# Dense products walked from the last column to the first: moving operand and PSUM bank with a step of -1

## The chip, the cores and the metric

The kernel runs on one core of a Trainium2 chip. The metric is the device time of one execution in microseconds (us), the median of the runs of a kernel. Of the core's engines, TensorE multiplies (PE in the profile's rows; PEld is its loading of weights), VectorE is DVE, ScalarE is ACT, GpSimd is POOL, and SyncE (SP) starts the DMAs.

## The reference

The reference is a two-layer encoder trunk over 512 tokens of 1024 features with 16 learned tokens put in front, 528 in all. Each layer is wrapped by two feed-forward networks with half a residual each:

```python
def swiglu(x, w_gate, w_up, w_down):
    return (jax.nn.silu(x @ w_gate) * (x @ w_up)) @ w_down
...
for layer in range(DEPTH):
    h = h + FFN_RESIDUAL * swiglu(rmsnorm(h, norm_ff1[layer]), ff1_w_gate[layer], ...)
    hn = rmsnorm(h, norm_mix[layer])
    # layer 0: z = hn @ w_in; gated short convolution || diagonal state-space model + GLU; concat @ w_out
    # layer 1: qkv = hn @ w_qkv; sliding-window attention, 16 query heads over 4 key heads; @ w_o
    h = h + mix
    h = h + FFN_RESIDUAL * swiglu(rmsnorm(h, norm_ff2[layer]), ff2_w_gate[layer], ...)
```

The feed-forward weights are 1024 x 2816 and 2816 x 1024, everything is float32, and the last layer drops the 16 learned tokens.

## The kernel before

**Layout.** Activations lie with features on the 128 partitions and tokens along the free dimension: `h`, `xh`, `xl` hold 8 feature tiles of 528 tokens, `act_h` and `act_l` 12. A row of `xh`, `xl`, `act_h`, `act_l` is 576 elements of 4 bytes, of which 528 are used. A value is kept as a rounded part (`xh`, `act_h`, `wh`) and the rest (`xl`, `act_l`, `wl`), in the type `float32r`, and a product is three matmuls: high weights by high values, high weights by low values, low weights by high values (the loop over `q`). `float32r` products go through TensorE once; the few products of plain float32 tiles are built as more than one pass.

**One dense product.** The weights are the stationary operand, a block of 128 x 128. The moving operand is a row of tokens, and the result goes to a bank of `ps`, the 8 banks of 512 float32. There are three choices of columns: `ALL` is two halves of 264 tokens in two banks, with the loop over `hf` inside the loop over `q`, so that halves alternate; `REAL` is the 512 real tokens at column 16; `FRONT` is 512 at column 0, where the operands of the last feed-forward network lie. A chain over the feature tiles adds into the same bank, then the last matmul raises `tile_full`. Every matmul loads its weights again, so there is one LDWEIGHTS record for each MATMUL record.

**Where they are.** `mm3` (its matmul is line 799) does nearly all of the four feed-forward networks: gate, up and down products. Lines 844 and 859 are the first two products of the kernel, issued while the inputs are still being split. Line 1015 is the input projection of layer 0, line 1029 its GLU, line 1057 its output projection, line 1126 the query projection of layer 1, lines 1227 and 1265 its output projection. The key and value projection (line 1076) has tokens as the stationary operand and weights as the moving one. Transposes, token sums, the state-space and the attention matmuls have lines of their own.

**What sets the order.** All is written out by hand, with semaphores. SP loads weight units of 16 blocks into one of two halves of `raw`; ACT rounds them to `wh` (line 1276), DVE takes the difference `wl` (line 1563); PE waits for `wl_ready`, for the banks' `tile_evac` and for `x_ready` or `act_ready`. DVE multiplies the finished banks by the norm (lines 1616, 1619) or adds them to `h` (line 1599), reading them forwards.

Of the kernel before, what the change touches and what calls it, by code (L numbers as in the profile page):

```python
# [25 lines left out]
P = 128  # L26
# [6 lines left out]
def trunk_program(nc, a, out, stop=None):  # L33
# [3 lines left out]
    L = META + SEQ  # L37
    KD = DM // P
# [4 lines left out]
    KC = DC // P  # L43
# [24 lines left out]
    GLU = (MIX[0] + 2 * KC, MIX[1] + 4 * KC)  # L68
# [21 lines left out]
    with ExitStack() as ctx:  # L90
# [170 lines left out]
        def span(col):  # L261
            c0, nh, nb = col
            return slice(c0, c0 + nb * nh)

        def operand(col):

# [522 lines left out]
        def _(pe):  # L789
            def mm3(pair, slot, blocks, x_h, x_l, k0, col, before_last=None, n_last=1):  # L790

                c0, nh, nb = col
                n = len(blocks)
                for k, b in enumerate(blocks):
                    if k == n - n_last and before_last:
                        before_last()
                    for q, (w, x) in enumerate(((wh, x_h), (wh, x_l), (wl, x_h))):
                        for hf in range(nb):
                            last = nc.tensor.matmul(ps[:, 2 * pair + hf, 0:nh], w[:, slot, b * P:(b + 1) * P],  # L799
                                                    x[:, k0 + k, c0 + hf * nh:c0 + (hf + 1) * nh],  # L800
                                                    start=(k == 0 and q == 0), stop=(k == n - 1 and q == 2))
                return last

# [28 lines left out]
            def first_job(col):  # L832

                c0, nh, nb = col
                pe.wait_ge(gate_split[0], 1)
                for k in range(KD):
                    pe.wait_ge(xh_done, k + 1)
                    for q, (w, x) in enumerate(((wh, xh), (wh, xl), (wl, xh))):
                        if q == 1:
                            pe.wait_ge(x_ready, k + 1)  # L840
                        if q == 2 and k in (0, EARLY):
                            pe.wait_ge(gate_split[1], 1 if k == 0 else 2)
                        for hf in range(nb):
                            last = nc.tensor.matmul(ps[:, hf, 0:nh], w[:, 0, k * P:(k + 1) * P], x[:, k, c0 + hf * nh:c0 + (hf + 1) * nh],  # L844
                                                    start=(k == 0 and q == 0), stop=(k == KD - 1 and q == 2))
                last.then_inc(tile_full, 1)

            def second_job(col):

                c0, nh, nb = col  # L850
                pe.wait_ge(wh_ready, 1)
                for k in range(KD):
                    if k == KD // 2:
                        first_scale()
                    for q, (w, x) in enumerate(((wh, xh), (wh, xl), (wl, xh))):
                        if k == 0 and q == 2:
                            pe.wait_ge(wl_ready, 1)
                        for hf in range(nb):
                            last = nc.tensor.matmul(ps[:, 2 + hf, 0:nh], w[:, 0, (KD + k) * P:(KD + k + 1) * P], x[:, k, c0 + hf * nh:c0 + (hf + 1) * nh],
                                                    start=(k == 0 and q == 0), stop=(k == KD - 1 and q == 2))  # L860
                last.then_inc(tile_full, 1)

# [136 lines left out]
            for p in range(4 * KC):  # L999
                stages(2 * p)  # L1000
                if p % 2 == 0:
                    pe.wait_ge(wl_ready, MIX[0] + p // 2 + 1)
                pe.wait_ge(tile_evac, MIX[1] + p - 1)
                if p == 0:
                    pe.wait_ge(x_ready, KD + KD - 1)
                slot = (MIX[0] + p // 2) % 2
                for k in range(KD):
                    if k == KD // 2:
                        stages(2 * p + 1)
                    if p == 0 and k == KD - 1:  # L1010
                        pe.wait_ge(x_ready, KD + KD)
                    b = p % 2 * KD + k
                    for q, (w, x) in enumerate(((wh, xh), (wh, xl), (wl, xh))):
                        for hf in range(2):
                            last = nc.tensor.matmul(ps[:, 2 * (p % 2) + hf, 0:L // 2], w[:, slot, b * P:(b + 1) * P], x[:, k, hf * L // 2:(hf + 1) * L // 2],  # L1015
                                                    start=(k == 0 and q == 0), stop=(k == KD - 1 and q == 2))
                last.then_inc(tile_full, 1)
                if p == 0:
                    token_sums(1, ALL)
# [3 lines left out]
            def glu_blocks(j, k0, k1):  # L1023

                for k in range(k0, k1):
                    b = k * KC + j
                    for q, (w, x) in enumerate(((wh, act_h), (wh, act_l), (wl, act_h))):
                        for hf in range(2):
                            last = nc.tensor.matmul(ps[:, 2 * (j % 2) + hf, 0:L // 2], w[:, GLU[0] % 2, b * P:(b + 1) * P], x[:, 2 * KC + k, hf * L // 2:(hf + 1) * L // 2],
                                                    start=(k == 0 and q == 0), stop=(k == KC - 1 and q == 2))  # L1030
                return last

# [11 lines left out]
            for d in range(KD):  # L1044
                if d % 2 == 0:
                    pe.wait_ge(wl_ready, WOUT[0] + d // 2 + 1)
                pe.wait_ge(tile_evac, WOUT[1] + d - 1)
                if d == 0:
                    pe.wait_ge(ya_ready, KC)
                slot = (WOUT[0] + d // 2) % 2  # L1050
                for k in range(KD):
                    if d == 0 and k >= KC:
                        pe.wait_ge(yb_ready, k - KC + 1)
                    b = d % 2 * KD + k
                    for q, (w, x) in enumerate(((wh, act_h), (wh, act_l), (wl, act_h))):
                        for hf in range(2):
                            last = nc.tensor.matmul(ps[:, 2 * (d % 2) + hf, 0:L // 2], w[:, slot, b * P:(b + 1) * P], x[:, k, hf * L // 2:(hf + 1) * L // 2],  # L1057
                                                    start=(k == 0 and q == 0), stop=(k == KD - 1 and q == 2))
                last.then_inc(tile_full, 1)
            ffn(1, ALL)  # L1060
# [49 lines left out]
            def query_part(g, t, half, sums=None):  # L1110

                slot = (u0 + g) % 2
                if half == 0:
                    if t == 0 and g == 2:
                        pe.wait_ge(half_low, 1)
                    elif t == 0 or g == 2:
                        pe.wait_ge(wl_ready, u0 + 2 + g + 1)
                    if g:
                        pe.wait_ge(tile_evac, j0 + 2 * g + t - 1)
                        if t == 1:  # L1120
                            pe.wait_ge(hn_var, g)
                c0, width, _ = REAL
                for k in range(half * KD // 2, (half + 1) * KD // 2):
                    b = t * KD + k
                    for q, (w, x) in enumerate(((wh, xh), (wh, xl), (wl, xh))):
                        last = nc.tensor.matmul(ps[:, 2 + t, :], w[:, slot, b * P:(b + 1) * P], x[:, k, c0:c0 + width],  # L1126
                                                start=(k == 0 and q == 0), stop=(k == KD - 1 and q == 2))
                    if sums is not None:
                        at = 2 * (k - half * KD // 2)
                        query_sums(sums, at, at + 2)  # L1130
                if half:
                    last.then_inc(tile_full, 1)
# [79 lines left out]
            def out_part(d, k0, k1, sums=None):  # L1212

                c0, width, _ = FRONT
# [9 lines left out]
                for k in range(k0, k1):  # L1224
                    b = d % 2 * KD + k
                    for q, (w, x) in enumerate(((wh, act_h), (wh, act_l), (wl, act_h))):
                        last = nc.tensor.matmul(ps[:, 2 + d, :], w[:, (WO[0] + d // 2) % 2, b * P:(b + 1) * P], x[:, k, c0:c0 + width],  # L1227
                                                start=(k == 0 and q == 0), stop=(k == KD - 1 and q == 2))
                    if sums is not None:
                        query_sums(sums, NT * (k - k0), NT * (k - k0 + 1))  # L1230
# [24 lines left out]
            for d in range(4, KD):  # L1255
# [5 lines left out]
                for k in range(KD):  # L1261
                    b = d % 2 * KD + k
                    block = lambda w, w3: w3[:, b // 4, b % 4 * P:(b % 4 + 1) * P] if d < 6 else w[:, (WO[0] + d // 2) % 2, b * P:(b + 1) * P]
                    for q, (w, x) in enumerate(((block(wh, w3h), act_h), (block(wh, w3h), act_l), (block(wl, w3l), act_h))):
                        last = nc.tensor.matmul(ps[:, d - 4, :], w, x[:, k, c0:c0 + width], start=(k == 0 and q == 0), stop=(k == KD - 1 and q == 2))  # L1265
                last.then_inc(tile_full, 1)
            ffn(3, REAL)

# [822 lines left out]
```

## Time and profile before

| | |
|---|---|
| median of 3 runs | 1881.0 us (1880.8 to 1881.09) |
| the profiled execution | 1882.0 us |
| its span, first to last instruction | 1880.0 us |
| PE busy | 1865.3 us, 13887 matmul records |
| PEld busy | 1765.6 us, 13887 records |
| DVE, ACT, POOL busy | 955.1, 599.6, 350.8 us |
| DMA | 188.29 MB, mean 100 GB/s |

How to read it: busy time is the union of an engine's records. A matmul's record lasts longer than the distance to the next one's start, since they are pipelined and their ends are modelled. So where a question is how fast matmuls follow each other, it is the number of starts in a stretch, or the start times, that answers. The granted clock is the share of TensorE's full 2.4 GHz that it had.

### The profile page before, as it was taken

What the parts mean: (1) busy time and instruction counts of PE and PEld (TensorE: products, weight loads), DVE (VectorE), ACT (ScalarE), POOL (GpSimd) and SP (SyncE); (2) the same over time, 40 slices, a digit from 0 to 9 for tenths busy, and PEclk for the clock granted to TensorE, in tenths of its full rate; (3) what the DMA queues carried; (4) which work ended last, traced back from release to release, by engine and by line L of the source; (5) the groups of instructions that cost most, each with busy time, mean ns of one, the idle gap of its engine ahead of it and who ended that gap; (6) DMA issues with size and microseconds to landing.
All of it is one profiled execution on the core that took longest, in us unless ns stands there. A gap on an engine that the chain in (4) does not pass through costs nothing.

```text
span 1880.0 us, 33855 instructions
## 1 busy us (share of the span) xinstructions
PE 1865.3 (99%) x13887; PEld 1765.6 (94%) x13887; DVE 955.1 (51%) x1077; ACT 599.6 (32%) x707; POOL 350.8 (19%) x629
## 2 busy tenths in 40 slices
PE   8999999999999999999999999999999999999999
PEld 8999999999999999999999999999988788888887
DVE  5444356568765443344564443445556654434443
ACT  5222222332243222222342222223456442222232
POOL 2888889414330000000000000000012000000000
PEclk9999999999999999999999999999999999999999
DMA  7332444547523332433243323322321233333423
GB/s 183 90 84 84 142 147 128 163 126 185 137 69 90 90 84 84 120 82 83 70 126 90 84 84 101 90 81 71 112 73 46 62 96 92 92 94 104 110 70 87
DMA packets 330785, 188.29 MB, mean 100 GB/s; under 512 B 8152, under 2 KB 323832, under 8 KB 330712
## 3 DMA queue, kind: packets, MB, share of 16 engines
q1 hardware_dynamic: 323296, 166.81, 32.0%
q0 software_dynamic: 7088, 20.38, 4.0%
q8 instruction: 52, 0.85, 0.2%
q14 instruction: 21, 0.17, 0.0%
q10 hardware_dynamic: 328, 0.07, 0.0%
HBM read 174.91 MB, written 11.14 MB: 99 GB/s over the span
## 4 chain that ended last, share of the span: by engine, by line
PE 95%; DVE 2%; issue 1%; ACT 1%; DMA 1%; ACTq 0%; POOL 0%; SPq 0%; DVEq 0%
PE ps L799 78%; PE ps L1015 5%; PE ps L1057 2%; PE ps L1126 2%; PE ps L1076 1%; PE ps L1265 1%; PE ps L1227 1%; DMA raw<-in_ff_w_down 1%; PE ps L844 1%; PE ps L1167 0%; PE ps L976 0%; PE ps L975 0%; PE ps L966 0%; DVE r L1592 0%; DVE wl L1563 0%
## 5 line engine op out<-in xcount | busy, mean ns | idle before, releaser
L799 PE MATMUL ps<-xh,wh 128*128 128x264 f32 (+1 forms) x2432 | 557.7, 299 | 0.3 <-DVE t_a L1616 0.2
L799 PE MATMUL ps<-xh,wl 128*128 128x264 f32 (+1 forms) x2432 | 556.6, 298 | 0.0
L799 PE MATMUL ps<-xl,wh 128*128 128x264 f32 (+1 forms) x2432 | 556.6, 298 | 0.0
L1563 DVE TENSOR_TENSOR wl<-raw,wh 128x2048 fp32r<-128x2048 f32 x171 | 398.3, 2329 | 173.6 <-ACT wh L1276 173.6
L1276 ACT ACTIVATE wh<-raw 128x2048 fp32r<-128x2048 f32 x172 | 327.5, 1904 | 248.6 <-PE ps L799 205.7
L799 PEld LDWEIGHTS ps<-xh,wh 128*128 128x128 f32 x2432 | 384.9, 188 | 15.3 <-issue 1.4
L799 PEld LDWEIGHTS ps<-xl,wh 128*128 128x128 f32 x2432 | 384.8, 188 | 13.8 <-issue 0.2
L799 PEld LDWEIGHTS ps<-xh,wl 128*128 128x128 f32 x2432 | 384.8, 188 | 13.8
L799 PE MATMUL ps<-act_h,wh 128*128 128x264 f32 (+1 forms) x1232 | 282.2, 298 | 1.2 <-DVE wl L1563 1.2
L799 PE MATMUL ps<-act_h,wl 128*128 128x264 f32 (+1 forms) x1232 | 281.6, 298 | 0.0
L799 PE MATMUL ps<-act_l,wh 128*128 128x264 f32 (+1 forms) x1232 | 281.5, 298 | 0.0
L1619 DVE TENSOR_TENSOR t_c<-ps,r 128x528 f32<-128x528 f32 (+1 forms) x88 | 61.9, 704 | 358.3 <-PE ps L799 356.5
L799 PEld LDWEIGHTS ps<-act_h,wh 128*128 128x128 f32 x1232 | 194.8, 188 | 8.2 <-issue 1.4
L799 PEld LDWEIGHTS ps<-act_h,wl 128*128 128x128 f32 x1232 | 194.8, 188 | 7.0
L799 PEld LDWEIGHTS ps<-act_l,wh 128*128 128x128 f32 x1232 | 194.9, 188 | 6.6
L1316 ACT ACTIVATE act_h<-t_c 128x528 f32 (+3 forms) x88 | 56.5, 642 | 447.8 <-DVE t_c L1622 447.8
L326 POOL TENSOR_TENSOR arena<-arena 128x32 f32<-128x32 f32 (+6 forms) x253 | 183.1, 724 | 19.6
L676 POOL TENSOR_SCALAR arena<-arena 128x16 f32<-128x16 f32 x4 | 1.0, 258 | 871.6 <-DVE arena L1948 842.3
L1314 ACT ACTIVATE t_bs<-t_a 128x528 f32<-128x528 f32 (+1 forms) x88 | 56.5, 643 | 274.6 <-DVE t_a L1616 274.6
L1599 DVE SCALAR_TENSOR_TENSOR h<-ps,h 128x528 f32 (+2 forms) x72 | 50.6, 703 | 182.0 <-PE ps L799 174.9
L1624 DVE TENSOR_TENSOR act_l<-t_c,act_h 128x528 f32 (+3 forms) x88 | 65.8, 747 | 78.5 <-ACT act_h L1316 78.5
L1622 DVE TENSOR_TENSOR t_c<-t_c,t_bs 128x528 f32<-128x528 f32 (+1 forms) x88 | 68.0, 773 | 9.0
(308 smaller groups left out, 1681.3 us busy)
## 6 DMA issues: line engine op xcount, KB each, us to landing
raw<-in_ff_w_gate SPq DMA_DIRECT2D x88, 512.0 KB, 4.0
raw<-in_ff_w_up SPq DMA_DIRECT2D x87, 512.0 KB, 5.2
raw<-in_ff_w_down SPq DMA_DIRECT2D x64, 384.0 KB, 4.0
raw<-in_ff_w_down SPq DMA_DIRECT2D x64, 320.0 KB, 3.7
raw<-in_even_w_in SPq DMA_DIRECT2D x16, 512.0 KB, 5.3
raw<-in_attn_w_qkv SPq DMA_DIRECT2D x12, 512.0 KB, 4.4
raw<-in_even_w_out SPq DMA_DIRECT2D x8, 512.0 KB, 4.5
raw<-in_attn_w_o SPq DMA_DIRECT2D x8, 512.0 KB, 4.6
```

The source lines that it names most:

```text
L326: did(g.tensor_tensor(o, x, y, op))
L799: last = nc.tensor.matmul(ps[:, 2 * pair + hf, 0:nh], w[:, slot, b * P:(b + 1) * P], x[:, k0 + k, c0 + hf * nh:c0 + (hf + 1) * nh], start= ...
L1015: last = nc.tensor.matmul(ps[:, 2 * (p % 2) + hf, 0:L // 2], w[:, slot, b * P:(b + 1) * P], x[:, k, hf * L // 2:(hf + 1) * L // 2], start= ...
L1057: last = nc.tensor.matmul(ps[:, 2 * (d % 2) + hf, 0:L // 2], w[:, slot, b * P:(b + 1) * P], x[:, k, hf * L // 2:(hf + 1) * L // 2], start= ...
L1276: nc.scalar.activation(wh[:, c % 2, :], raw[:, c % 2, :], ACT.Copy).then_inc(wh_ready, 1)
L1314: nc.scalar.activation(t_b[:, cols], t_a[:, cols], ACT.Silu).then_inc(silu_done[n], 1)
L1316: nc.scalar.activation(act_h[:, s + 2 * i, span(operand(col))], t_c[:, cols], ACT.Copy).then_inc(act_h_done[n], 1)
L1563: v.tensor_tensor(wl[:, c % 2, :], raw[:, c % 2, :], wh[:, c % 2, :].bitcast(F32), ALU.subtract).then_inc(wl_ready, 1)
L1599: v.scalar_tensor_tensor(hd, tile(pair, col), scale, hd, ALU.mult, ALU.add).then_inc(tile_evac, 1)
L1619: v.tensor_tensor(halves(t_c, col), tile(1, col), halves(r, col), ALU.mult).then_inc(tile_evac, 1)
L1622: v.tensor_tensor(t_c[:, cols], t_c[:, cols], t_b[:, cols], ALU.mult).then_inc(gated[n], 1)
L1624: v.tensor_tensor(act_l[:, s + 2 * i, span(operand(col))], t_c[:, cols], act_h[:, s + 2 * i, span(operand(col))].bitcast(F32), ALU.subtrac ...
```

## The change

A function `backwards` turns the last dimension of a two-dimensional slice round. It is put on the result and on the moving operand of the matmuls of lines 799, 844, 859, 1015, 1029, 1057, 1126, 1227 and 1265 (of before). Since both are turned, each result lands where it landed. The stationary operands, line 1076 and all other matmuls, and every other engine's code are as they were. In the program that is built, the last dimension of these two operands reads step -1, count 264 or 512, with an offset at the last element, where it read step 1 and an offset at the first. On each engine the same instructions stand in the same order.

```diff
+        def backwards(ap):
+
+            return ap[:, ::-1]
+
...
                         for hf in range(nb):
-                            last = nc.tensor.matmul(ps[:, 2 * pair + hf, 0:nh], w[:, slot, b * P:(b + 1) * P],
-                                                    x[:, k0 + k, c0 + hf * nh:c0 + (hf + 1) * nh],
+                            last = nc.tensor.matmul(backwards(ps[:, 2 * pair + hf, 0:nh]), w[:, slot, b * P:(b + 1) * P],
+                                                    backwards(x[:, k0 + k, c0 + hf * nh:c0 + (hf + 1) * nh]),
                                                     start=(k == 0 and q == 0), stop=(k == n - 1 and q == 2))
...
-                        last = nc.tensor.matmul(ps[:, 2 + t, :], w[:, slot, b * P:(b + 1) * P], x[:, k, c0:c0 + width],
+                        last = nc.tensor.matmul(backwards(ps[:, 2 + t, :]), w[:, slot, b * P:(b + 1) * P], backwards(x[:, k, c0:c0 + width]),
                                                 start=(k == 0 and q == 0), stop=(k == KD - 1 and q == 2))
```

The other seven places are changed in the same way.

## Rows read from the trace of the kernel before

**Rows 1.** The page: busy us (share) xinstructions, and granted clock in 40 slices.

```profile
PE 1865.3 (99%) x13887; PEld 1765.6 (94%) x13887; DVE 955.1 (51%) x1077; ACT 599.6 (32%) x707; POOL 350.8 (19%) x629
...
PEclk9999999999999999999999999999999999999999
```

**Rows 2.** The page: the chain that ended last, by line.

```profile
PE ps L799 78%; PE ps L1015 5%; PE ps L1057 2%; PE ps L1126 2%; PE ps L1076 1%; PE ps L1265 1%; PE ps L1227 1%; DMA raw<-in_ff_w_down 1%; PE ps L844 1%; PE ps L1167 0%; PE ps L976 0%; PE ps L975 0%; PE ps L966 0%; DVE r L1592 0%; DVE wl L1563 0%
```

**Rows 3.** PE's waits, longest first: us in total, times, longest us.

```profile
PE ps L916 <- DMA arena<-in_meta_tokens: 3.0, 1, 3.0
PE ps L844 <- ACT xh L1288: 2.7, 1, 2.7
```

**Rows 4.** Two stretches: us, PE, PEld, DVE, ACT, POOL busy (xstarts), clock, DMA.

```profile
600.00:900.00 300.00, 300.00 (x2503) 300.00 (x2502) 124.70 (x117) 77.26 (x68) 0.00 (x0) 1.00 0.32 89
...
1600.00:1800.00 200.00, 200.00 (x884) 165.62 (x883) 85.65 (x79) 54.35 (x46) 0.00 (x0) 1.00 0.34 94
```

**Rows 5.** PE's groups by shape: xcount | busy us, mean ns | idle before.

```profile
L799 PE MATMUL ps<-xh,wh 128*128 128x264 f32 x2080 | 420.3, 283 | 0.1
...
L799 PE MATMUL ps<-act_h,wh 128*128 128x264 f32 x1056 | 213.1, 283 | 1.2 <-DVE wl L1563 1.2
...
L799 PE MATMUL ps<-xh,wh 128*128 128x512 f32 x352 | 137.5, 391 | 0.2 <-DVE t_a L1616 0.2
...
L799 PE MATMUL ps<-act_h,wh 128*128 128x512 f32 x176 | 69.1, 393 | 0.0
...
L1015 PE MATMUL ps<-xh,wh 128*128 128x264 f32 x256 | 53.3, 290 | 0.5 <-DVE arena L1751 0.5
...
L1126 PE MATMUL ps<-xh,wh 128*128 128x512 f32 x64 | 26.6, 415 | 0.0
L1057 PE MATMUL ps<-act_h,wh 128*128 128x264 f32 x128 | 25.8, 284 | 0.3 <-DVE act_l L1854 0.3
...
L1227 PE MATMUL ps<-act_h,wh 128*128 128x512 f32 x32 | 14.0, 436 | 0.0
...
L1029 PE MATMUL ps<-act_h,wh 128*128 128x264 f32 x32 | 6.6, 288 | 0.3 <-ACT t_bs L1430 0.3
...
L1265 PE MATMUL ps<-act_h 128*128 128x512 f32 x16 | 6.2, 389 | 0.0
...
L844 PE MATMUL ps<-xh,wh 128*128 128x264 f32 x16 | 4.6, 380 | 2.7 <-ACT xh L1288 2.7
...
L859 PE MATMUL ps<-xh,wh 128*128 128x264 f32 x16 | 3.3, 290 | 0.0
```

**Rows 6.** The timeline of PE early on: start us, us of the pair, what.

```profile
18.65 0.65 PE L844 MATMUL ps<-xh,wl 128*128 128x264 f32 x2
19.09 0.65 PE L844 MATMUL ps<-xh,wh 128*128 128x264 f32 x2
...
21.94 0.40 PE L844 MATMUL ps<-xh,wl 128*128 128x264 f32 x2
22.18 0.40 PE L844 MATMUL ps<-xh,wh 128*128 128x264 f32 x2
```

**Rows 7.** The timeline of PE: 512 columns of line 799, then of line 1126.

```profile
1639.82 0.39 PE L799 MATMUL ps<-xl,wh 128*128 128x512 f32 x1
1640.05 0.39 PE L799 MATMUL ps<-xh,wl 128*128 128x512 f32 x1
1640.27 0.39 PE L799 MATMUL ps<-xh,wh 128*128 128x512 f32 x1
...
1384.47 0.39 PE L1126 MATMUL ps<-xl,wh 128*128 128x512 f32 x1
...
1385.85 0.39 PE L1126 MATMUL ps<-xl,wh 128*128 128x512 f32 x1
```

**Rows 8.** The timeline of PE at float32 products, and line 1140's shape.

```profile
26.50 1.05 PE L932 MATMUL ps<-t_c,ones 128*128 128x128 f32 x8
27.48 0.39 PE L933 MATMUL ps<-t_bs,ones 16*128 16x16 f32 x2
...
L1140 PE MATMUL ps<-pair_ones,t_bs 128*128 128x2 f32 x64 | 7.8, 238 | 0.0
```

More of the change, by code:

```diff
@@ L843, in first_job @@
                         for hf in range(nb):
-                            last = nc.tensor.matmul(ps[:, hf, 0:nh], w[:, 0, k * P:(k + 1) * P], x[:, k, c0 + hf * nh:c0 + (hf + 1) * nh],
+                            last = nc.tensor.matmul(backwards(ps[:, hf, 0:nh]), w[:, 0, k * P:(k + 1) * P], backwards(x[:, k, c0 + hf * nh:c0 + (hf + 1) * nh]),
                                                     start=(k == 0 and q == 0), stop=(k == KD - 1 and q == 2))
@@ L858, in second_job @@
                         for hf in range(nb):
-                            last = nc.tensor.matmul(ps[:, 2 + hf, 0:nh], w[:, 0, (KD + k) * P:(KD + k + 1) * P], x[:, k, c0 + hf * nh:c0 + (hf + 1) * nh],
+                            last = nc.tensor.matmul(backwards(ps[:, 2 + hf, 0:nh]), w[:, 0, (KD + k) * P:(KD + k + 1) * P], backwards(x[:, k, c0 + hf * nh:c0 + (hf + 1) * nh]),
                                                     start=(k == 0 and q == 0), stop=(k == KD - 1 and q == 2))
@@ L1014, in _ @@
                         for hf in range(2):
-                            last = nc.tensor.matmul(ps[:, 2 * (p % 2) + hf, 0:L // 2], w[:, slot, b * P:(b + 1) * P], x[:, k, hf * L // 2:(hf + 1) * L // 2],
+                            last = nc.tensor.matmul(backwards(ps[:, 2 * (p % 2) + hf, 0:L // 2]), w[:, slot, b * P:(b + 1) * P], backwards(x[:, k, hf * L // 2:(hf + 1) * L // 2]),
                                                     start=(k == 0 and q == 0), stop=(k == KD - 1 and q == 2))
@@ L1028, in glu_blocks @@
                         for hf in range(2):
-                            last = nc.tensor.matmul(ps[:, 2 * (j % 2) + hf, 0:L // 2], w[:, GLU[0] % 2, b * P:(b + 1) * P], x[:, 2 * KC + k, hf * L // 2:(hf + 1) * L // 2],
+                            last = nc.tensor.matmul(backwards(ps[:, 2 * (j % 2) + hf, 0:L // 2]), w[:, GLU[0] % 2, b * P:(b + 1) * P], backwards(x[:, 2 * KC + k, hf * L // 2:(hf + 1) * L // 2]),
                                                     start=(k == 0 and q == 0), stop=(k == KC - 1 and q == 2))
@@ L1056, in _ @@
                         for hf in range(2):
-                            last = nc.tensor.matmul(ps[:, 2 * (d % 2) + hf, 0:L // 2], w[:, slot, b * P:(b + 1) * P], x[:, k, hf * L // 2:(hf + 1) * L // 2],
+                            last = nc.tensor.matmul(backwards(ps[:, 2 * (d % 2) + hf, 0:L // 2]), w[:, slot, b * P:(b + 1) * P], backwards(x[:, k, hf * L // 2:(hf + 1) * L // 2]),
                                                     start=(k == 0 and q == 0), stop=(k == KD - 1 and q == 2))
@@ L1226, in out_part @@
                     for q, (w, x) in enumerate(((wh, act_h), (wh, act_l), (wl, act_h))):
-                        last = nc.tensor.matmul(ps[:, 2 + d, :], w[:, (WO[0] + d // 2) % 2, b * P:(b + 1) * P], x[:, k, c0:c0 + width],
+                        last = nc.tensor.matmul(backwards(ps[:, 2 + d, :]), w[:, (WO[0] + d // 2) % 2, b * P:(b + 1) * P], backwards(x[:, k, c0:c0 + width]),
                                                 start=(k == 0 and q == 0), stop=(k == KD - 1 and q == 2))
@@ L1264, in _ @@
                     for q, (w, x) in enumerate(((block(wh, w3h), act_h), (block(wh, w3h), act_l), (block(wl, w3l), act_h))):
-                        last = nc.tensor.matmul(ps[:, d - 4, :], w, x[:, k, c0:c0 + width], start=(k == 0 and q == 0), stop=(k == KD - 1 and q == 2))
+                        last = nc.tensor.matmul(backwards(ps[:, d - 4, :]), w, backwards(x[:, k, c0:c0 + width]), start=(k == 0 and q == 0), stop=(k == KD - 1 and q == 2))
                 last.then_inc(tile_full, 1)
```

## The prediction

> **What bounds the kernel now.** Start with the page's busy times and its slices: PE is busy 1865.3 us of a span of 1880.0, and the granted clock stands at full speed, 2.4 GHz, in all 40 slices [rows 1]. Busy time alone says little, since records of pipelined matmuls overlap, so the chain that ended last comes next: 78% of the span is line 799, and lines 1015, 1057, 1126, 1265, 1227 and 844 stand in it too [rows 2]. PE's waits agree: the longest is 3.0 us and comes before the first transpose [rows 3]. So TensorE sets the end, and nearly everything it does is the dense products whose operands the diff turns round. Whatever a dense matmul gains or loses goes into the end uncovered; the other engines wait for PE, and no slack takes it up.
>
> What one matmul costs is the pitch, the time from one start to the next, not the 283 or 390 ns that a record lasts. Two long stretches without any other PE work give it by count [rows 4]: 2503 starts of 264 columns in 300 us are 119.9 ns each; 884 starts of 512 columns in 200 us are 226.2 ns each.
>
> How many there are comes from the groups by shape [rows 5]. Each row shown is one of three of the same size (high by high, low by high, high by low), except that line 1265 has six. 264 columns: 3 x (2080 + 1056 + 256 + 128 + 32 + 16 + 16) = 10752. 512 columns: 3 x (352 + 176 + 64 + 32) + 6 x 16 = 1968. Together 12720 matmuls, 10752 x 119.9 ns = 1289 us plus 1968 x 226.2 ns = 445 us: 1734 us, 92% of the span, lies under the edit. The key and value product of line 1076, the transposes, the state-space and attention matmuls are as before.
>
> **The change part by part.** The edit adds no instruction and no wait and moves nothing in any queue. Each of the 12720 matmuls keeps its shape, weights, bank, wait and place. What changes is the step of two of its operands, from +1 to -1, and their first address, from the lowest to the highest of the same 264 or 512 elements. There are four places where that could cost or give something.
>
> (a) Order against the neighbours. Both the read and the bank are reversed, so column c still meets weight column by weight column what it met before and lands at its old address. Two successive adds to the same column are still one pitch apart (two pitches where two halves alternate), since every matmul of a chain walks the same way. The semaphore is raised by the last matmul's end, and VectorE, which is behind PE by whole tiles, sees the same moment. DMA, SyncE, VectorE and ScalarE do what they did. Cost nil; if this were wrong it would show as a wait of PE, and the longest today after the start is below 3 us [rows 3].
>
> (b) Rate while columns stream. At the full clock a column takes 1/2.4 = 0.417 ns, at the lower level 1/1.2 = 0.833 ns. The first matmuls of the kernel run at the lower level: pairs of 264 start 0.44 us apart, 220 ns each, exactly 264 x 0.833 [rows 6]. The later ones run in pairs 0.24 us apart. If a backward walk can be served only at one element where two are served now, a matmul would have the lower level's pitch: 220 instead of 119.9, and 512 x 0.833 = 426.7 instead of 226.2. That is the upper bound: 10752 x 100.1 + 1968 x 200.5 ns = 1076 + 395 = 1471 us. The lower bound is nil: a column cannot take less than 0.417 ns. I take nil. The trace has no backward operand to go by; the row that a backward matmul is nearest to is its own forward one, with the same elements at the same addresses, each next to the one before it, and that one loses 9.9 ns in 264 columns.
>
> (c) What each matmul costs beyond its columns. 264 columns need 110.0 ns and 512 need 213.3, so the surplus is 9.9 and 12.9 ns [rows 4], in all 10752 x 9.9 + 1968 x 12.9 ns = 106 + 25 = 132 us. At the lower clock it is hidden altogether [rows 6]. So something at each change of matmul takes a time of its own, and it may depend on where the operand starts: line 799's 512-column products, which start at column 0, have a pitch of 0.225 to 0.23 us (226.2 by count), while line 1126's, which start at column 16, show 1.38 us for six, 230 ns [rows 7]. That is 3.8 ns, and other things differ there too (the neighbouring work, the banks). Backwards, the start moves by 263 or 511 elements. The bounds by these rows: the surplus vanishes (-132 us) or doubles (+132 us); the address term of line 1126 on every matmul is 12720 x 3.8 ns = 48 us either way. I take nil, because line 799's 264-column halves start at column 0 and at column 264 and their pairs keep 0.24 us throughout, so most places of a start are alike. This is the weakest step: 0.3 ns per matmul, 12720 x 0.3 ns = 3.8 us, is already 0.2% of the time.
>
> (d) The number format. A pair of operands in full float32 instead of the kernel's rounded form shows two records per product of 128 columns: four products on line 932 take 0.98 us, 245 ns each [rows 8], 1.91 ns a column against 0.45 here. If the reversed step threw the products back to that form, the price would be milliseconds. The types of the tiles are untouched, and I keep this out of the sum and the range.
>
> What the Trainium skill says on (b) speaks both ways. "Advanced Engine Details and Errata", section Memory Cachelines, has it that PSUM works in lines of two fp32 values, that any non-contiguous pattern slows matmuls a good deal, and that every two consecutive elements should be contiguous; for SBUF it wants at least two hits on a 16-byte line. Read by lines, a backward walk fills them all as well as a forward one, and the sum is 1881; read to the letter, -1 is not contiguous, and the rival of the halved rate below holds. No row here decides: the only moving operand with another step, line 1140's, has two columns [rows 8], which says nothing of a rate.
>
> Sum: nil + nil + nil. The profiled execution took 1882.0 us, its span 1880.0 and 2.0 around it; the median of the three runs is 1881.0. The forecast is 1881.0.
>
> **The rivals.**
> *Halved rate (slower).* Reading or adding backwards is served singly: term (b) at its upper bound, 1881 + 1471 = 3352 us. For it: at full clock the operand must come twice as fast as at the lower level, and the trace shows only steps of +1 doing that. Against: each element is still next to the one before it. It decides at once; with even a tenth of this loss (10 ns on 264 columns) the kernel would be at 2028.
>
> *A dearer start (slower).* Each matmul pays more where one follows another: between the address term, 1881 + 48 = 1929, and the doubled surplus, 1881 + 132 = 2013. For it: the surplus exists, and it differs between lines 799 and 1126. Against: it is nearly the same for 264 columns starting at two different places and for 512. It decides from 0.3 ns per matmul.
>
> *A cheaper start (faster).* The same term with the other sign; half the address term gives 1881 - 24 = 1857, all of the surplus 1749. For it only that the surplus is there to be had.
>
> *The change doesn't do what it says.* Both steps are reversed in each product, so something on the way to the engine could fold them back. The time would be 1881.0 and nothing in it could tell this from the forecast.
>
> **How the numbers follow.** Within 0.2% (which is about what a measurement of this kernel can tell from no change): no effect 0.54, folded back 0.03, together 0.57. Dearer start 0.17. Halved rate or something else beyond 2015 us 0.17. Cheaper start 0.09. So faster 0.09, same 0.57, slower 0.34. To hold 8 in 10 the range takes in the forecast, the dearer start up to its doubled surplus and the smaller part of the cheaper one: 1850 to 2015. The halved rate stays outside. Signs are not evenly split, so no second range is needed.
>
> **What the profile of the changed kernel would show.** If right: 2503 starts in a 300 us stretch of 264 columns and 884 in a 200 us stretch of 512, the full clock, line 799 at 78% of the chain, the same 3.0 us as PE's longest wait. A dearer or cheaper start shows as another pitch in the full-clock stretches with the 0.44 us of the low-clock pairs kept. A halved rate shows there as 220 and 427 ns, with VectorE and ScalarE waiting more for line 799 and no new wait of PE. If 264 and 512 columns lose the same number of ns, the start is dearer; if they lose in the ratio of their columns, the rate is. What would make the prediction wrong is one number, a pitch that moved by more than 0.3 ns.

## The result, and the profile after

The changed kernel takes 1904.3 us (median of 4 runs, 1903.6 to 1904.7) against 1881.05 for the kernel before, run again beside it: a ratio of 1.0122, with a 95% interval of 1.0105 to 1.0140. It is 23.2 us slower. The profiled execution took 1903.59 us, its span 1901.6, 21.6 us more than before.

The page of the changed kernel first: PE's busy line, the granted clock, and the chain that ended last by line. They answer to [rows 1] and [rows 2]; its line numbers are 4 higher.

```profile
PE 1888.3 (99%) x13887; PEld 1777.0 (93%) x13887; DVE 955.8 (50%) x1077; ACT 599.5 (32%) x707; POOL 349.8 (18%) x629
...
PEclk9999999999999999999999999999999999999999
...
PE ps L803 79%; PE ps L1019 5%; PE ps L1061 2%; PE ps L1130 2%; PE ps L1080 1%; PE ps L1269 1%; PE ps L1231 1%; PE ps L1171 1%; PE ps L1192 0%; PE ps L1182 0%; PE ps L980 0%; PE ps L979 0%; PE ps L970 0%; PE ps L848 0%; PE ps L863 0%
```

The counts are the same, the clock is full, the other engines' busy times are within 1 us of what they were, and PE grew by 23 us. Its waits (us in total, times, longest) are also those of before, against [rows 3]:

```profile
PE ps L920 <- DMA arena<-in_meta_tokens: 3.0, 1, 3.0
PE ps L848 <- ACT xh L1292: 2.6, 1, 2.6
```

So the time is in the matmuls themselves. The same two stretches as in [rows 4], now of the changed kernel (us, PE, PEld, DVE, ACT, POOL busy and starts, clock, DMA):

```profile
600.00:900.00 300.00, 300.00 (x2479) 300.00 (x2478) 123.65 (x115) 75.04 (x67) 0.00 (x0) 1.00 0.32 89
1600.00:1800.00 200.00, 200.00 (x859) 161.15 (x858) 83.09 (x76) 51.50 (x43) 0.00 (x0) 1.00 0.34 94
```

264 columns start every 300/2479 = 121.0 ns (119.9 before), 512 columns every 200/859 = 232.8 (226.2 before): 1.1 to 1.2 ns and 6.6 ns more. These counts take in two or three matmuls whose records reach over the edges of a stretch. From the first to the last start inside the same stretches it is 120.0 and 226.7 ns before, 121.1 and 233.3 after: the same differences, and the figures to hold against the rates further down. The timeline of PE shows the latter directly, 0.233 us from start to start against 0.225 to 0.23 in [rows 7]:

```profile
1649.77 0.40 PE L803 MATMUL ps<-xh,wh 128*128 128x512 f32 x1
1650.01 0.40 PE L803 MATMUL ps<-xl,wh 128*128 128x512 f32 x1
1650.24 0.40 PE L803 MATMUL ps<-xh,wl 128*128 128x512 f32 x1
```

Following the first starts through both timelines gives where the 21.6 us of span arise. The first matmul of line 799 (803) begins at 30.79 before and 29.70 after; the key and value product at 1343.97 and 1353.11; the last feed-forward network at 1511.68 and 1523.33; its last dense matmul at 1874.91 and 1896.52. The 264-column part therefore lost 9.1 + 1.1 = 10.2 us, where 10656 matmuls x 1.1 ns are 11.7; the 1.2 us wait for `wl` on line 799 [rows 5] is gone from the changed kernel's waits and accounts for most of the rest. The last network lost 10.0 us, its 1584 x 6.6 ns = 10.4. Layer 1's mixer lost 2.5 us, but not as 384 matmuls x 6.6 ns: the 192 matmuls of line 1126, which read from column 16, went from 229.4 to 233.4 ns, 4.0 each, and 0.9 us of the 2.5 stands in attention matmuls (lines 1167, 1168 and 1188) that the change doesn't touch. So the loss lies on the dense matmuls, by width and also by where their rows start. With these terms 10752 x 1.1 + 1776 x 6.6 + 192 x 4.0 ns = 24.3 us; less the wait of 1.2 that is 23.1, against 23.2 measured.

### The profile page after: what moved, and what is told of

Same layout as the page of the kernel before. It is cut to its first block, busy times and chain, and to the rows that moved or that the text cites. A ratio compares the mean times of both kernels' runs of the same rounds, so it can differ in the third digit from the quotient of the medians.

```text
span 1901.6 us, 33855 instructions
## 1 busy us (share of the span) xinstructions
PE 1888.3 (99%) x13887; PEld 1777.0 (93%) x13887; DVE 955.8 (50%) x1077; ACT 599.5 (32%) x707; POOL 349.8 (18%) x629
## 4 chain that ended last, share of the span: by engine, by line
PE 97%; DVE 1%; issue 1%; ACT 1%; ACTq 0%; POOL 0%
PE ps L803 79%; PE ps L1019 5%; PE ps L1061 2%; PE ps L1130 2%; PE ps L1080 1%; PE ps L1269 1%; PE ps L1231 1%; PE ps L1171 1%; PE ps L1192 0%; PE ps L1182 0%; PE ps L980 0%; PE ps L979 0%; PE ps L970 0%; PE ps L848 0%; PE ps L863 0%
## 5 line engine op out<-in xcount | busy, mean ns | idle before, releaser
L803 PE MATMUL ps<-xh,wh 128*128 128x264 f32 (+1 forms) x2432 | 563.5, 302 | 0.0
L1286 ACT ACTIVATE t_bs<-h 128x528 f32 (+1 forms) x40 | 25.7, 643 | 145.8 <-DVE h L1603 127.2
```

The source lines that it names most:

```text
L803: last = nc.tensor.matmul(backwards(ps[:, 2 * pair + hf, 0:nh]), w[:, slot, b * P:(b + 1) * P], backwards(x[:, k0 + k, c0 + hf * nh:c0 + ( ...
```

## The experiments

### One operand at a time

The change's two halves were undone in turn. In the first kernel only the moving operand keeps its step of -1, in the second only the banks do (shortened):

```diff
-nc.tensor.matmul(backwards(ps[...]), w[...], backwards(x[...]), ...)
+nc.tensor.matmul(ps[...], w[...], x[..., ::-1], ...)        # moving_only
+nc.tensor.matmul(ps[..., ::-1], w[...], x[...], ...)        # bank_only
```

> The changed kernel with the banks walked forwards again; only the moving operand keeps its step of -1. Columns of a result land mirrored, so what is computed differs; the work is the same in kind and number. In the changed kernel a matmul of 264 columns starts every 121.0 ns (2479 starts in 300 us) against 119.9 before, one of 512 every 232.8 ns (859 in 200 us) against 226.2. Theory A, the read of the moving operand is what is dearer backwards: both pitches stay at 121.0 and 232.8 and the time at 1904 us. Theory B, the write into the bank is what is dearer: pitches 119.9 and 226.2, time 1881 us. Theory C, both share it: in between, and the two runs' losses add up to 23 us.

Measured: 1903.88 us, ratio 1.0118 (1.0102 to 1.0135). Its two stretches:

```profile
600.00:900.00 300.00, 300.00 (x2479) 300.00 (x2479) 123.06 (x114) 75.85 (x67) 0.00 (x0) 1.00 0.32 89
1600.00:1800.00 200.00, 200.00 (x859) 161.15 (x858) 82.29 (x75) 51.85 (x44) 0.00 (x0) 1.00 0.34 95
```

> The changed kernel with the moving operand forwards again; only the banks are walked backwards. Columns of a result land mirrored. Theory A (the read is dearer): pitches 119.9 and 226.2 ns, 1881 us. Theory B (the write is dearer): 121.0 and 232.8 ns, 1904 us. Theory C (both): in between.

Measured: 1881.36 us, ratio 0.9999 (0.9989 to 1.0009). Its two stretches:

```profile
600.00:900.00 300.00, 300.00 (x2502) 300.00 (x2501) 124.74 (x116) 77.26 (x68) 0.00 (x0) 1.00 0.32 89
1600.00:1800.00 200.00, 200.00 (x884) 165.59 (x883) 85.58 (x79) 53.57 (x46) 0.00 (x0) 1.00 0.35 95
```

The starts are 2479 and 859 in one, 2502 and 884 in the other. Theory A holds outright: the whole loss is in the read of the moving operand, and a bank costs the same walked either way.

### Two widths at a time

```diff
         def backwards(ap):
 
-            return ap[:, ::-1]
+            return ap[:, ::-1] if ap.shape[1] == 512 else ap    # wide_only; != 512 in narrow_only
```

> The change on the 1968 matmuls of 512 columns alone; the 10752 of 264 columns are as before. What is computed is as in the kernel before. Theory L (the loss is a local cost of each matmul, 6.6 ns at 512 columns and 1.1 ns at 264): 1881 + 1968 x 6.6 ns = 1894 us, and line 799's stretches of 264 columns back at 119.9 ns. Theory G (the loss comes from somewhere else, such as a wait or a transfer shifted early in the kernel): anything but 1894, and stretches of 264 columns not back at 119.9.

> The change on the 10752 matmuls of 264 columns alone; the 1968 of 512 are forwards. What is computed is as before. If every loss is local to its matmul (theory L), this and the run with the 512-column products alone add up to the whole change: 23.2 - 11.3 = 12 us, so 1893 us, with 121.1 ns in stretches of 264 columns and 226.7 in those of 512. If losses are not local (theory G) the two parts don't add up.

Measured: 1892.95 us for the 512-column products alone (ratio 1.0062, 1.0045 to 1.0079) and 1891.84 for the 264-column ones alone (1.0058, 1.0040 to 1.0076), 11.3 and 10.5 us. Together they are 21.8 against 23.2 for both, well inside the intervals (0.0017 of 1881 is 3 us). The sums that were expected, 13.0 and 11.8 us, are 1.7 and 1.3 us above what each lost. Each leaves the other width alone. The stretch of 264 columns of the first and that of 512 columns of the second:

```profile
600.00:900.00 300.00, 300.00 (x2502) 300.00 (x2501) 124.83 (x116) 77.20 (x68) 0.00 (x0) 1.00 0.32 89
```

```profile
1600.00:1800.00 200.00, 200.00 (x884) 165.62 (x883) 85.75 (x79) 54.63 (x46) 0.00 (x0) 1.00 0.34 95
```

The loss is local. But 1.1 ns at 264 columns and 6.6 at 512 is neither one price for each matmul nor one for each column.

### Rates, measured with TensorE alone

Three kernels leave the trunk out. Each ran once, at the full clock, and has 68 to 81 stretches like this one (shortened), with one thing varied in each:

```python
for c in range(2):
    for k in range(8):
        for q, (w, x) in enumerate(((wh, xh), (wh, xl), (wl, xh))):
            nc.tensor.matmul(ps[0:M, c % 4, 0:n], w[:, k * P + w0:k * P + w0 + M], x[:, k, c0:c0 + n], ...)
```

> Not the trunk: 68 stretches of 48 matmuls each with TensorE alone at work, on 128 x 128 weights, the three products of high and low parts as in line 799, nothing computed of the reference. It varies one thing at a time: direction of the moving operand and of the bank, 128 to 512 columns, the first column (0, 1, 2, 4, 8, 16, 32, 48, 64, 264), one or several banks, the step (2), float32r or bfloat16, the same weights or the same moving row again. Theory A: every stretch with a backward moving operand is dearer, those with a backward bank alone are not; theory B the other way round. Theory P (the price is of where the walk starts, not of its direction): a forward walk from some other first column has the pitch of the backward one, about 233 ns at 512 columns. Theory N (the price grows with columns): the gap between backward and forward grows in step from 128 to 512, from some 0.5 to 6.6 ns; if the price is of one matmul, the gap is one number at all widths, which 1.1 ns at 264 and 6.6 at 512 already speak against.

The chain that ended last of this kernel (start us, us, what) lists each stretch by its line. Lines 77, 83, 89, 95 are halves of 264 columns, with moving operand and bank walked forwards-forwards, forwards-backwards, backwards-forwards and both backwards; lines 101, 107, 113, 119 are the same four for 512:

```profile
58.47 11.52 PE ps L77 x96
69.99 11.52 PE ps L83 x96
81.51 11.63 PE ps L89 x96
93.14 11.63 PE ps L95 x96
104.77 10.93 PE ps L101 x48
115.70 10.88 PE ps L107 x48
126.58 11.21 PE ps L113 x48
137.78 11.20 PE ps L119 x48
```

Divided by the count: 120.0, 120.0, 121.1, 121.1 ns and 227.7, 226.7, 233.5, 233.3. The trunk's pitches appear with no other engine at work, and again only the moving operand's direction counts. The same view where the first column of a forward walk of 512 is 16 (line 221), 32 (line 233) and 48 (line 245):

```profile
295.81 10.99 PE ps L221 x48
...
318.00 11.15 PE ps L233 x48
...
340.35 11.20 PE ps L245 x48
```

That is 229.0, 232.3 and 233.3 ns for forward walks; from column 8 it is 233.3 too, from 1 even 236.9, and from 64 the 227.7 of column 0. (The forward stretch from column 0 has 227.7 ns here and 226.7 in the two other kernels, so a single stretch repeats to about 1 ns.) The backward walk costs 233.3 to 233.5 from each of them whose first column is a multiple of 4, and 235.6 from columns 1 and 2. So theory P is right as far as it goes: a forward walk pays as much as a backward one when it starts elsewhere. What is special is the place where the kernel before reads, not the reversal. Theory N is not met. The gap tends to grow with the columns, but not in step: from start to start the backward chain lost 1.1 ns at 128 columns, gained 0.6 at 192, 2.0 at 256 and 1.3 at 264, lost 1.6 at 288 and 2.2 at 304, nothing at 320 and 368, 2.0 at 352 and 400, 4.2 at 384 and 416, 1.2 at 464, 6.4 at 496 and 5.6 at 512, 6.7 against the 226.7 (these widths are from this kernel and the third).

Other stretches settle the remaining theories. Bfloat16, 512 columns, forwards (line 431) and with the moving operand backwards (line 443); bfloat16, 256 columns, with step 1 (line 383), the moving operand in step 2 (line 389) and the bank in step 2 (line 395); float32r, 256 columns, the moving operand in step 2 (line 377):

```profile
524.56 10.89 PE ps L377 x48
535.45 5.26 PE ps L383 x48
540.71 5.44 PE ps L389 x48
546.15 10.36 PE ps L395 x48
...
588.47 10.36 PE ps L431 x48
...
609.19 10.36 PE ps L443 x48
```

Bfloat16 has 215.8 ns in both directions, 2.5 ns over its columns: of the two formats measured, only float32r shows the effect. A halved rate does exist, but for a step of 2: 226.9 ns for 256 float32r columns (120.4 with step 1, line 293), and, in bfloat16, 215.8 for 256 columns into a bank in step 2 (109.6 with step 1). A bfloat16 moving operand in step 2 pays only a little, 113.3 ns. The Trainium skill ("Advanced Engine Details and Errata", Memory Cachelines) says that a non-contiguous pattern in PSUM slows matmuls a good deal; by that rule, the bank in step 2 agrees, and a bank in step -1, which costs nothing (226.7 ns, line 107), can't count as non-contiguous.

> Not the trunk: stretches of TensorE alone as in the first measurement of rates. It varies the number of weight columns loaded (128, 96, 64, 32), the first column of the weights (0 to 64) with the moving operand from column 0, both shifted alike, weights with step 2, and pairs of 264 columns with the halves in other places and directions. Theory W (the 13.3 ns beyond the columns are time that the load of the next weights takes from the moving read): the surplus at 512 columns falls in proportion to the weight columns, from 13.3 ns at 128 to 3 to 4 ns at 32, the gap of 6.6 ns of the backward walk shrinks with it, and shifting the weights by 8 columns costs what shifting the moving operand did (about 6.6 ns), while shifting both alike costs nothing. Theory S (a fixed cost of starting a matmul in this number format, with its own price for a start in the middle of a memory line): neither surplus nor gap depends on the weights' columns or place.

The chain of this kernel: with 32 weight columns, 512 columns forwards (line 165) and backwards (line 170); then 512 columns forwards from column 0 with the weights begun 16 (line 235) and 48 (line 255) elements later; then both begun 16, 32 and 48 later (lines 305, 315, 325):

```profile
185.57 11.11 PE ps L165 x48
196.69 11.20 PE ps L170 x48
...
314.67 11.20 PE ps L235 x48
...
359.74 11.00 PE ps L255 x48
...
471.65 10.91 PE ps L305 x48
...
493.77 10.93 PE ps L315 x48
...
515.90 10.93 PE ps L325 x48
```

One prediction of theory W fell: with a quarter of the weights, the backward walk still takes 233.3 ns and the forward one 231.5, more than the 226.7 with all of them. The gap does shrink, from 6.6 ns to 1.9, but because the forward walk gets dearer. The surplus is not the length of the weights' load. The other held: weights 16 later cost what the moving operand 48 later did (233.3), weights 48 later what the moving operand 16 later did (229.2 and 229.0), and both moved alike, by 16, 32 or 48, are back at 227.3 to 227.7. Theory S, that neither place matters to the other, falls with it. But moving both alike gives the time back only for steps like these. Both begun 1, 2 or 4 elements later (lines 275, 285, 295), the forward walk takes 237.9, 233.3 and 231.3 ns:

```profile
404.07 11.42 PE ps L275 x48
...
426.84 11.20 PE ps L285 x48
...
449.35 11.10 PE ps L295 x48
```

So below 8 elements (32 bytes) an operand's own place counts too. Weights in step 2 also take the good pitch away, with 233.3 ns forwards.

> Not the trunk: stretches of TensorE alone. First column of the moving operand or of the weights 0 to 56 by 8, for 512 columns and for halves of 264, forwards and backwards; bfloat16 from four first columns; walks of both directions in turn; 272 to 480 columns. Theory Q: moving operand from column s and weights from column 64 - s give the same forward pitch; both moved alike give that of column 0; bfloat16 stays at 215.8 ns everywhere. The backward gap, 0 at 320 columns, 4.4 at 384, 6.6 at 512, takes whole steps of 16 cycles (6.67 ns) on a part of the matmuls. Theory U (only the moving operand's place counts): no pitch changes with the weights' place.

The chain of this kernel, 512 columns forwards: the moving operand from column 16 (line 141), the weights from 48 (line 278); then backwards with the weights from 32 (line 217):

```profile
197.50 11.01 PE ps L141 x48
...
482.74 11.00 PE ps L278 x48
...
356.95 11.20 PE ps L217 x48
```

The whole series, worked out from the first and last starts of each stretch, in ns:

| place of the moving operand less that of the weights, modulo 64 | 0 | 8 | 16 | 24 | 32 | 40 | 48 | 56 |
|---|---|---|---|---|---|---|---|---|
| 512 forwards, moving operand shifted | 226.7 | 233.4 | 229.4 | 233.3 | 232.2 | 234.3 | 233.4 | 233.2 |
| 512 forwards, weights shifted | 226.7 | 233.3 | 229.1 | 233.2 | 233.3 | 234.0 | 233.3 | 233.4 |
| 512 backwards, weights shifted | 233.4 | 233.5 | 233.3 | 233.3 | 233.3 | 233.3 | 233.3 | 233.3 |
| halves of 264 forwards, moving operand shifted | 120.3 | 120.8 | 122.1 | 123.4 | 123.3 | 120.2 | 120.2 | 120.3 |
| halves of 264 backwards, moving operand shifted | 121.1 | 121.6 | 121.7 | 122.8 | 121.6 | 121.1 | 121.2 | 123.3 |
| halves of 264 forwards, both shifted (by 0 to 56) | 120.0 | 120.0 | 120.0 | 120.1 | 120.1 | 120.1 | 120.1 | 120.0 |

The two ways of getting the same difference agree within 0.3 ns in seven of eight columns and 1.1 ns in the eighth, and moving both alike by multiples of 8 costs nothing. Bfloat16 had 215.8 ns from columns 8, 32 and 48 and 216.7 from column 1, in both directions. At 512 columns, the difference of 0 is the one good place of the eight, and a walk backwards has none. At 264, three other places are as good as 0.

Theory Q's last part, whole steps of 6.67 ns, is not met below 512 columns: at 384 the distances between starts went from 173 to 174 ns forwards to 175 to 176 and 181 to 182 backwards, at 400 from 180 to 182 and 183. And a matmul's own direction is not all: with forward and backward walks of 512 in turn, a pair takes 466.7 ns, 233.3 a matmul, and not the mean of 226.7 and 233.3.

### Back in the trunk: the same loss without a reversal

If this is the cause, walks that are all forwards must lose as much when only their place is changed, and get it back when the weights follow. Three kernels, of the kernel before (`xl`, `act_h` and `act_l` are changed as `xh` is):

```diff
-        xh = sb("xh", [P, KD, ROW], F32R)[:, :, 0:L]
+        xh = sb("xh", [P, KD, ROW], F32R)[:, :, 8:8 + L]     # shifted_rows; 32:32 + L in rows_by_32 and both_by_32
...
+        sb("pad", [P, 32])                                    # both_by_32: 128 bytes ahead of wh and wl
         wh = sb("wh", [P, 2, UNITW], F32R)
```

> The kernel before, all walks forwards, with the rows of xh, xl, act_h and act_l begun 8 elements (32 bytes) later in their 576; what is computed is as before. The measured rates gave a forward walk of 512 columns from column 8 a pitch of 233.3 ns, that of the backward walk, against 226.7 from column 0. Theory P (what counts is where in memory the walk lies against the weights' read, and backwards is one more way to lie badly): the 512-column products lose as much as in the changed kernel, 1968 x 6.6 ns = 13 us, at least 1892 us, and the 264-column ones lose between nothing and 1.1 ns more. Theory R (only the reversed direction costs): 1881 us.

Measured: 1898.84 us, ratio 1.0089 (1.0071 to 1.0107). Its stretches have 2485 and 859 starts, 120.7 and 232.8 ns: 10752 x 0.8 + 1968 x 6.6 ns = 8.6 + 13.0 = 21.6 us, against 17.5 measured. The profiled execution, from which the starts are, was the slowest of the four, 1902.6 us, 21.3 above the kernel before; the others took 1895.7 to 1899.7. Why these times lie further apart than those of the kernel before (1880.7 to 1882.3) is open.

```profile
600.00:900.00 300.00, 300.00 (x2485) 300.00 (x2484) 123.64 (x115) 75.71 (x67) 0.00 (x0) 1.00 0.32 89
1600.00:1800.00 200.00, 200.00 (x859) 160.67 (x858) 83.58 (x76) 51.70 (x44) 0.00 (x0) 1.00 0.34 94
```

> The kernel before, all walks forwards, with the rows of the moving operands (xh, xl, act_h, act_l) begun 32 elements (128 bytes) later; what is computed is as before. Theory Q (the pitch depends on where the moving read lies against the weights' read, counted modulo 64 elements): by the rates measured with TensorE alone, 232.3 ns at 512 columns and 123.3 for halves of 264 from column 32, so 1881 + 1968 x 5.6 ns + 10752 x 3.3 ns = 1881 + 11 + 35 = 1927 us. Theory R (only direction costs): 1881 us.

Measured: 1923.13 us, ratio 1.0216 (1.0194 to 1.0237), against 1927 worked out from the rates. Its four executions also lie apart, 1918.3 to 1926.6. It is slower than the reversal.

```profile
600.00:900.00 300.00, 300.00 (x2433) 299.88 (x2433) 124.12 (x114) 76.77 (x68) 0.00 (x0) 1.00 0.33 90
1600.00:1800.00 200.00, 200.00 (x862) 162.15 (x861) 83.56 (x76) 51.71 (x44) 0.00 (x0) 1.00 0.34 94
```

> As the run with the rows 32 elements later, with 128 bytes of unused memory put before the weights' tiles wh and wl, so that they lie 32 elements later too; what is computed is as before. Theory Q: moving operand and weights stand against each other as in the kernel before, 226.7 and 119.9 ns, 1881 us. Theory U (what counts is the moving operand's own place in memory, not that against the weights): 1927 us, as with the rows alone.

Measured: 1881.16 us, ratio 0.9998 (0.9989 to 1.0008). One unused tile of 128 bytes takes back all 42 us:

```profile
600.00:900.00 300.00, 300.00 (x2502) 300.00 (x2501) 124.69 (x116) 77.25 (x68) 0.00 (x0) 1.00 0.32 89
1600.00:1800.00 200.00, 200.00 (x884) 165.62 (x883) 85.67 (x80) 54.66 (x46) 0.00 (x0) 1.00 0.34 93
```

> The changed kernel, backwards everywhere it was, with 128 bytes of unused memory before wh and wl, so that the weights lie 32 elements later. With TensorE alone a backward walk of 512 columns had 240.0 ns against weights begun 32 elements later, and 233.3 at every other place measured. Theory Q: line 799's 512 columns go from 233.3 to 240.0 ns, 1904 + 1968 x 6.7 ns = 1917 us, plus what the 264 columns change (not yet measured, between nothing and 3.3 ns each, up to 35 us). If the trunk's weights or rows lay otherwise than those of the measured rates: 1904 us.

Measured: 1909.34 us, ratio 1.0148 (1.0131 to 1.0164); this is the changed kernel with the same unused tile.

```profile
600.00:900.00 300.00, 300.00 (x2468) 300.00 (x2467) 123.69 (x115) 77.29 (x68) 0.00 (x0) 1.00 0.32 87
1600.00:1800.00 200.00, 200.00 (x859) 161.16 (x858) 82.89 (x75) 51.41 (x43) 0.00 (x0) 1.00 0.34 95
```

The number that this expectation rested on was not met. The 512-column pitch stayed at 232.8 ns, and in the third kernel of rates the same shift gave 233.3, where the second had shown 240.0; in the second, rows were 576 elements long, in the third 640. The trunk's rows are 576 too, so that length alone doesn't explain it; what made the 240.0 is open. The 264-column pitch rose from 121.0 to 121.6 ns (2468 starts), 10752 x 0.6 ns = 6 us, against 5.1 us measured over the changed kernel. So the place of the weights matters to a backward walk too, at 264 columns; with the moving operand 32 later instead, the rates have the same 121.6.

One product that was never walked backwards bears the rule out, since its operands moved with the rows and weights. In the key and value product (line 1076) the weights are the moving operand, from their first element, and the tokens, from column 16, the stationary one: a difference of -16, which is 48. PE's timeline, six matmuls apart, in the kernel before and then with the rows 32 elements later, where the difference becomes 16:

```profile
1347.22 0.40 PE L1076 MATMUL ps<-wl,xh 128*128 128x512 f32 x1
...
1348.62 0.40 PE L1076 MATMUL ps<-wl,xh 128*128 128x512 f32 x1
```

```profile
1379.19 0.39 PE L1076 MATMUL ps<-wl,xh 128*128 128x512 f32 x1
...
1380.57 0.39 PE L1076 MATMUL ps<-wl,xh 128*128 128x512 f32 x1
```

Over 91 distances the means are 233.1 and 229.2 ns, and 234.0 with the rows 8 later (a difference of 40). The table's row for shifted weights has 233.3, 229.1 and 234.0. So the same edit that slowed the trunk by 42 us made this product faster.

## Why the prediction was wrong

**The bound, the counts and the absence of cover** were right. 12720 matmuls lie on the path, no other engine entered it, and a difference of about a nanosecond each came through in full; the one thing that took something up was a single wait of 1.2 us.

**Step (a)**, order and banks, was right; with the banks alone reversed the time is 1881.36 us.

**The number.** The forecast was no change, 1881.0 us, and 1904.3 lies inside the range of 1850 to 2015 only because the range took in the rival of a dearer start. It lies below that rival's own lower end of 1929.

**Step (b)** was right that the rate isn't halved. Its reason, that each element is still next to the one before it, fits the measured step of -1 and, for float32r, step of 2, but it then took the surplus as untouched, which is step (c).

**Step (c) failed.** It took nil for the change of place because line 799's halves start at column 0 and 264 and still run at 0.24 us a pair, "so most places of a start are alike". That row couldn't carry it: read to 0.01 us a pair, it can't show 1 ns a matmul, and it holds both halves in one. The rates show the contrary: of eight places at 512 columns only one has 226.7 ns, and six have 232 to 234, and at 264 the places differ by 3 ns. In place of nil, the change of walk cost 6.6 ns at 512 columns (4.0 from column 16) and 1.1 at 264. The row that said so was in hand: line 1126, from column 16, at 230 ns [rows 7], was put down to possible neighbours and banks; with TensorE alone, column 16 costs 228.9 to 229.4. Taken at its 3.8 ns for every matmul it gave 48 us, the lower end of the dearer start; the true terms are 6.6 ns at 512 columns but 1.1 at 264, 12.5 + 11.8 = 24.3 us, and 23.2 measured. The mechanism of that rival was the nearest, and its size was too large because one number stood for both widths. The prediction gave that rival 0.17, and 0.54 to no effect. The 0.3 ns threshold was right, and it should have warned: a forecast of no change claimed that a price of 10 ns, seen to vary by 3.8, would stay within 0.3.

**The rule for telling start from rate** in the last part (equal ns, or ns in the ratio of columns) fitted neither: 1.1 and 6.6 ns have a ratio of 6 at twice the columns. **Step (d)** and the rivals of a halved rate, of a cheaper start and of an edit without effect are excluded by the pitches.

What stays open is why. The runs show that the pitch depends on the place of the two reads against each other, modulo 64 elements (256 bytes), and on the moving read's direction; the weights were never reversed. They don't show what of the memory the two share, why an operand's own place counts below 8 elements, nor why the forward walk gets dearer with fewer weight columns. A kernel with the weights' read turned round wasn't tried.

## What to carry to other kernels

Where TensorE's stream is the bound and operands are float32r, the place of the moving operand against the weights is worth a look: here 2.2% hung on 128 bytes, 1.2% on the direction, and neither shows as a wait or in a busy share, only in starts per stretch. Start rows and weight blocks at the same place modulo 256 bytes, and both at a multiple of 32 bytes: that was the best place at 512 columns and as good as any at halves of 264. Check the pitch with TensorE alone before believing an edit of an access pattern is free. A bank may be walked backwards for nothing; a step of 2 halved the rate in the bank (bfloat16) and in a float32r moving operand.

## What the runs showed of the hardware that was not expected

- Float32r matmuls with weights of 128 columns started 110.6 to 112.3 ns apart however few columns they had (128 to 240), and with 96 weight columns 84.5 to 85.0 ns, with 64 or 32 60.0 ns, all at 128 columns. The kernel's 264 columns at 120.0 ns stand just above that floor.
- Float32r has a surplus over its columns even at the best place, 10.0 ns at halves of 264 and 13.3 at 512, in the trunk as with TensorE alone, and up to 17 ns at widths between; bfloat16 has 2.5 at both. At the lower clock the trunk shows none [rows 6].
- The Trainium skill ("TensorE: Matmul & The Clock Gate", Step-by-step: what each phase is for) says that the moving read and the weights' load have independent ports, so that loading the next weights takes nothing from the running matmul. By that rule the weights' place could not matter. For float32r these runs don't agree: 226.7 to 234.0 ns by the weights' place alone. For bfloat16 nothing speaks against it (215.8 to 216.7 ns from four first columns and in both directions), but its weights were not shifted.
